# The recurrence's gate rows, made in eight pieces between the weight splits of the projection's second half

## The reference

```python
def mlstm_chunk_scan(q, k, v, li, lf, C0, n0, m0):      # per chunk of 128 tokens
        b = jnp.cumsum(fc, axis=-1)
        d_log = b[..., :, None] - b[..., None, :] + ic[..., None, :]
        inter_log = b + m[..., None]
        m_t = jnp.maximum(inter_log, jnp.max(d_log, axis=-1))
...
        m_new = m_t[..., -1]
        w = jnp.exp(b[..., -1:] - b + ic - m_new[..., None])
        decay = jnp.exp(b[..., -1] + m - m_new)
...
    li = g[:, 0]
    lf = jax.nn.log_sigmoid(g[:, 1])
```

## Time and profile before

| | |
|---|---|
| median of 3 runs | 1189.91 us (1189.72 to 1190.07) |
| profiled execution | 1190.76 us, span 1189.0 us |
| TensorE busy | 1041.1 us (88%) |
| VectorE busy | 669.0 us (56%) |
| ScalarE busy | 414.4 us (35%) |
| GpSimd busy | 202.3 us (17%) |
| mean granted TensorE clock | 0.935 of full speed |

### The profile page before, as it was taken

How to read it: one execution, slowest core, us unless ns; L and a number is a source line. 1 busy time by engine, 2 the same in 40 slices (tenths; PEclk the granted TensorE clock), 3 DMA queues, 4 the chain that set the end, 5 groups by cost and what they waited for, 6 DMA issues and landing times.

```text
span 1189.0 us, 18131 instructions
## 1 busy us (share of the span) xinstructions
PE 1041.1 (88%) x5952; PEld 795.1 (67%) x5953; DVE 669.0 (56%) x1128; ACT 414.4 (35%) x808; POOL 202.3 (17%) x244
## 2 busy tenths in 40 slices
PE   7999999999999988888878999983599999989950
PEld 3899999999999864668874555552366666556630
DVE  2544885231985158229985423357567676467644
ACT  3443222343222251546661110120344444244413
POOL 2010000000000030002363000000224443324324
PEclk9799999999999999699998999995699999989985
DMA  9634333313343132122126322217458888887839
GB/s 362 259 138 141 123 131 135 107 69 117 133 141 107 53 121 78 48 89 63 54 38 252 114 90 91 106 68 268 178 165 240 286 275 284 281 264 198 230 54 353
DMA packets 58644, 187.38 MB, mean 158 GB/s; under 512 B 7874, under 2 KB 20658, under 8 KB 52450
## 3 DMA queue, kind: packets, MB, share of 16 engines
q1 hardware_dynamic: 46820, 144.92, 34.1%
q0 software_dynamic: 7920, 28.84, 10.4%
q10 hardware_dynamic: 3856, 13.00, 2.9%
HBM read 151.53 MB, written 35.21 MB: 157 GB/s over the span
## 4 chain that ended last, share of the span: by engine, by line
PE 71%; DVE 13%; DMA 7%; issue 3%; ACT 3%; POOL 1%; ACTq 1%; SPq 0%; DVEq 0%; POOLq 0%
PE psum L1267 35%; PE psum L1209 28%; DMA RB<-in_w_exp 3%; DVE RW L1768 2%; PE psum L1486 2%; DMA RB<-in_x_sample 2%; DVE RE L1795 1%; PE psum L1132 1%; DMA acc_scratch<-RE,idxsc 1%; DMA out<-RB 1%; DVE RE L1803 1%; PE psum L1421 1%; PE psum L1224 1%; PE psum L1188 1%; DMA RW<-gm_scratch 1%
## 5 line engine op out<-in xcount | busy, mean ns | idle before, releaser
L1209 PE MATMUL psum<-input_parts,weight_parts 128*128 128x320 f32 x2208 | 342.4, 314 | 2.0 <-DVE input_parts L1591 2.0
L1209 PEld LDWEIGHTS psum<-input_parts,weight_parts 128*128 128x128 f32 x2208 | 328.4, 190 | 11.0 <-issue 6.9
L1267 PE MATMUL psum<-RB,RW 128*128 x324 | 146.5, 603 | 1.7 <-issue 1.1
L1598 DVE TENSOR_TENSOR weight_parts<-RW,weight_parts 128x1024 fp32r<-128x1024 f32 x46 | 56.3, 1224 | 155.4 <-ACT weight_parts L860 155.4
L860 ACT ACTIVATE weight_parts<-RW 128x1024 fp32r<-128x1024 f32 x46 | 48.6, 1057 | 232.8 <-PE psum L1209 232.8
L1267 PE MATMUL psum<-expert_parts 128*128 128x512 f32 x486 | 126.5, 414 | 1.9 <-DVE expert_parts L2032 1.9
L1267 PEld LDWEIGHTS psum<-expert_parts 128*128 128x128 f32 x486 | 91.3, 188 | 32.4 <-issue 14.5
L1267 PEld LDWEIGHTS psum<-RB,RW 128*128 128x128 f32 x324 | 60.7, 194 | 68.9 <-issue 68.9
L1267 PE MATMUL psum<-RS,RB 128*128 128x512 f32 (+1 forms) x200 | 79.9, 554 | 3.5 <-DMA RS<-in_wpw 2.3
L1267 PE MATMUL psum<-RC,RB 128*128 128x512 f32 x160 | 72.6, 608 | 0.0
L674 POOL TENSOR_TENSOR RE<-RE,RA 2x2304 f32<-2x2304 f32 (+1 forms) x2 | 9.5, 4762 | 361.6 <-DMA RA<-in_b_ada 361.6
(11 more groups left out here) (333 smaller groups left out, 1486.6 us busy)
## 6 DMA issues: line engine op xcount, KB each, us to landing
RB<-in_w_exp SPq DMA_DIRECT2D x48, 1024.0 KB, 7.9
RW<-in_w_in SPq DMA_DIRECT2D x46, 512.0 KB, 4.4
RW<-in_w_ada SPq DMA_DIRECT2D x34, 512.0 KB, 3.4
RA<-in_w_ada SPq DMA_DIRECT2D x10, 512.0 KB, 15.5
RW<-gm_scratch SPq DMA_DIRECT2D x20, 256.0 KB, 3.4
h_scratch<-RE SPq DMA_DIRECT2D x10, 512.0 KB, 2.6
acc_scratch<-RA SPq DMA_DIRECT2D x10, 512.0 KB, 3.6
RB<-acc_scratch ACTq DMA_DIRECT2D x10, 512.0 KB, 8.7
```

The source lines that it names most:

```text
L1209: last = nc.tensor.matmul(psum[:, 2 * r + g, 0:GW], spl[:, r, wv, k], hT[:, xv, k, g * GW:(g + 1) * GW], start=(k == 0 and wv == 0 and xv ...
L1267: return nc.tensor.matmul(out, lhsT, rhs, start=start, stop=stop, **kw_)
L1598: nc.vector.tensor_tensor(spl[:, r, 1], raw[:, r], spl[:, r, 0].bitcast(F32), ALU.subtract).then_inc(wlo_ok, 1)
```

## The change

The gate rows leave their place behind the projection. VectorE makes them in eight functions, each called between two low splits of the projection's second half; the convolution's taps start two splits later. Rows move to other memory, since their old places are in use then (`rowE`, `rowG` in the part of `RC` that later holds the second half's values, `rowF` in two slots of the projection's output, a new `rowW` in the place of the gated input). ScalarE makes the exponential and the logarithm after its second slot of the second half; it waits for all gate outputs before it evicts into `rowF`'s place, and for the stores before it writes over `rowE` and `rowG`. SP issues the stores ahead of the value chunks' weights and the load behind them. `gate_columns` stands after the second Fourier product of the sample, the second variance after the fourth. GpSimd waits for the centring as well. No step of the computation is added or left out.

```diff
@@ rows
-    rowF = RA[0:ROWG, 4 * T:5 * T]
-    rowG = RA[0:ROWG, 5 * T:6 * T]
-    rowE = RB[0:ROWG, (NSLOT + GT) * HT:(NSLOT + GT + 2) * HT]
+    rowE = RC[0:ROWG, va:va + T]
+    rowG = RC[0:ROWG, va + T:va + 2 * T]
+    rowF = RB[0:ROWG, (NSLOT + KK + 2) * HT:(NSLOT + KK + 4) * HT]
+    rowW = RB[0:ROWG, (NSLOT + GT) * HT:(NSLOT + GT + 2) * HT]
@@ sync: the six stores and the load of dec
+            if h == 1:
+                sp.wait_ge(gout, GOUT_ALL)
+                for d in range(2):
+                    sp.dma_start(gm_dram[d], rowG[32 * d:32 * d + NH, :]).then_inc(gm_out, 16)
...
             for c in range(V0, O0):
                 load_proj(None, (n0 + c) % 2, c, n0 + c - 1)
+            if h == 1:
+                sp.wait_ge(gm_out, 64)
+                sp.dma_start(dec[:, :, :, :].rearrange("p d h t -> p (d h t)"),
+                             dec_dram.rearrange("d h t -> (d h t)").partition_broadcast(P)).then_inc(dec_in, 16)
...
         sp.wait_ge(gtr_ps, 4)
+        sp.wait_ge(mrow_out, 48)
@@ gpsimd
+        gp.wait_ge(cen_ok, 4)
@@ scalar
+            if h == 1:
+                act.wait_ge(gstep, 10)
+                nc.scalar.activation(rowC, rowC, ACT.Exp, scale=-1.0).then_inc(gact, 1)
+                act.wait_ge(gact, 1)
+                nc.scalar.activation(rowC, rowC, ACT.Ln, bias=1.0).then_inc(gact, 1)
             with act.Fori(1, 3) as i:
...
+            if h == 1:
+                act.wait_ge(gout, GOUT_ALL)
+            for j in range(2):
+                slot(6, j)
...
+                if h == 1 and j == 0:
+                    act.wait_ge(gm_out, 64)
@@ tensor
-            for q, row in enumerate((LF, rowC, rowD, LI)):
+            for q, row in enumerate((LF, rowW, rowD, LI)):
...
         for i in range(TS // P):
-            if i == 6:
+            if i == 2:
                 gate_columns()
+            if i == 4:
                 variance(1)
@@ vector: the order
-        low(25, 32)
+        low(25, 26)
+        gate_logs()
+        low(26, 27)
+        gate_reversed()
+        low(27, 28)
+        gate_sums()
+        low(28, 29)
+        gate_maxima()
+        low(29, 30)
+        gate_forward()
+        low(30, 32)
         dve.wait_ge(gt_sig, 2)
         nc.vector.tensor_tensor(urest[:, :, 2 * PAD:2 * PAD + HT], PT[:, 1, CA:CA + 2], PT[:, 1, GT:GT + 2],
                                 ALU.mult).then_inc(u_ok, 1)
         dve.wait_ge(u_ok, 6)
+        gate_first()
+        low(32, 33)
+        gate_rest()
+        low(33, 34)
         first_tap(rest)
         for k in range(10):
             taps(rest, 4 * TAPS, 1 + 3 * k, 4 + 3 * k)
-            low(32 + k, 33 + k)
-        low(42, 2 * NCH)
+            low(34 + k, 35 + k)
+        low(44, 2 * NCH)
@@ vector: two of the eight pieces
+        def gate_sums():
+            link(nc.vector.memset(rowF, 1.0))
+            link(nc.vector.memset(rowF[:, 0:T:P], 0.0))
+            dve.wait_ge(gact, 2)
+            link(nc.vector.scalar_tensor_tensor(rowD, rowD, 0.0, rowC, ALU.min, ALU.subtract))
+            link(nc.vector.tensor_tensor_scan(rowC, rowF, rowD, 0.0, ALU.mult, ALU.add))
+
+        def gate_maxima():
+            dve.wait_ge(zero_out, 16)
+            link(nc.vector.tensor_tensor_scan(rowG[:, 0:TP], rowD[:, 0:TP], rowE[:, 0:TP], 0.0, ALU.add, ALU.max))
+            link(nc.vector.tensor_tensor_scan(rowG[:, TP:T], rowD[:, TP:T], rowE[:, TP:T], gvec[:, 2:3], ALU.add, ALU.max))
+            link(nc.vector.tensor_tensor(rowF, rowG, rowC, ALU.subtract))
+            link(nc.vector.tensor_tensor(rowE, rowE, rowC, ALU.subtract))
```

More of the change, by code:

```diff
@@ L417, in program @@
     GOUT_ALL = 19
+    GSTEPS = 25
     place = [2 * D, 0, 0]
@@ L524, in _ @@
         sp.dma_start(wr[:, :, :], a["w_router"]).then_inc(tab_in, 16)
-        sp.wait_ge(gout, GOUT_ALL)
-        for d in range(2):
-            sp.dma_start(gm_dram[d], rowG[32 * d:32 * d + NH, :]).then_inc(gm_out, 16)
-            sp.dma_start(dec_dram[d], small[32 * d:32 * d + NH, 3, :]).then_inc(gm_out, 16)
-            sp.dma_start(o[4][0, 0, d:d + 1, :].rearrange("a h -> h a"), small[32 * d:32 * d + NH, 2, 0:1],
-                         allow_slow_non_contiguous=True).then_inc(out_done, 16)
-        sp.wait_ge(gm_out, 64)
-        sp.dma_start(dec[:, :, :, :].rearrange("p d h t -> p (d h t)"),
-                     dec_dram.rearrange("d h t -> (d h t)").partition_broadcast(P)).then_inc(dec_in, 16)
         sp.wait_ge(gtr_ps, 4)
+        sp.wait_ge(mrow_out, 48)
         for d in range(2):
@@ L1611, in taps, with link @@
                                                    ALU.mult, ALU.add).then_inc(conv, 1)
+        steps = [0]
+        def link(ins):
+            steps[0] += 1
+            ins.then_inc(gstep, 1)
+            dve.wait_ge(gstep, steps[0])
+        SEQ = ((0, TP), (TP, T))
+        fw, bk = slice(0, NH), slice(32, 32 + NH)
+        mprev, mlast, decs, deco = (small[:, i, :] for i in range(4))
+        ch = lambda ap: ap.rearrange("p (c t) -> p c t", t=P)
+        per = lambda ap, r, c0, c1: ap[r, c0 // P:c1 // P].unsqueeze(2).broadcast_to([NH, (c1 - c0) // P, P])
@@ new lines, in gate_logs, with gate_reversed @@
+        def gate_logs():
+            dve.wait_ge(cm_ev, NCH + 1)
+            dve.wait_ge(gates_ev, 2)
+            dve.wait_ge(u_ok, 4)
+            link(nc.vector.memset(rowD, 0.0))
+            link(nc.vector.memset(rowE, 0.0))
+            link(nc.vector.tensor_copy(rowE[fw, :], LI[fw, :]))
+            link(nc.vector.tensor_scalar(rowD[fw, :], LF[fw, :], gvec[fw, 1:2], None, ALU.add))
+        def gate_reversed():
+            for c0, c1 in SEQ:
+                link(nc.vector.tensor_copy(rowE[bk, c0:c1][:, ::-1], LI[bk, c0:c1]))
+                link(nc.vector.tensor_scalar(rowD[bk, c0:c1][:, ::-1], LF[bk, c0:c1], gvec[bk, 1:2], None, ALU.add))
+            link(nc.vector.memset(rowC, 0.0))
+            link(nc.vector.scalar_tensor_tensor(rowC, rowD, -1.0, rowD, ALU.mult, ALU.max))
@@ new lines, in gate_first, with gate_rest @@
+        def gate_first():
+            link(nc.vector.memset(rowW, 0.0))
+            nc.vector.tensor_tensor(ch(rowW[fw, :]), per(mprev, fw, 0, T), ch(rowF[fw, :]), ALU.subtract).then_inc(gout, 1)
+            gate_backward(*SEQ[0])
+        def gate_rest():
+            gate_backward(*SEQ[1])
+            nc.vector.tensor_copy(deco[fw, :], decs[fw, :]).then_inc(gout, 1)
+            nc.vector.tensor_copy(deco[bk, 0:PT_TILES][:, ::-1], decs[bk, 0:PT_TILES]).then_inc(gout, 1)
+            nc.vector.tensor_copy(deco[bk, PT_TILES:][:, ::-1], decs[bk, PT_TILES:]).then_inc(gout, 1)
+            dve.wait_ge(gout, 15)
+            nc.vector.tensor_copy(decs[:, 0:1], rowG[:, TP - 1:TP]).then_inc(gout, 1)
+            dve.wait_ge(gout, 16)
+            nc.vector.tensor_scalar(rowG[fw, :], rowF[fw, :], -1.0, None, ALU.mult).then_inc(gout, 1)
+            for c0, c1 in SEQ:
+                nc.vector.tensor_scalar(rowG[bk, c0:c1][:, ::-1], rowF[bk, c0:c1], -1.0, None, ALU.mult).then_inc(gout, 1)
@@ L1713, in _ @@
-        link(nc.vector.tensor_tensor(rowF, rowG, rowC, ALU.subtract))
-        link(nc.vector.tensor_tensor(rowE, rowE, rowC, ALU.subtract))
-        mprev, mlast, decs, deco = (small[:, i, :] for i in range(4))
-        link(nc.vector.memset(mprev[:, 0:1], 0.0))
-        link(nc.vector.tensor_copy(mprev[:, 1:2], rowG[:, P - 1:P]))
-        link(nc.vector.tensor_copy(mprev[:, PT_TILES:PT_TILES + 1], gvec[:, 2:3]))
-        link(nc.vector.tensor_copy(mprev[:, PT_TILES + 1:NT], rowG[:, TP + P - 1:T - 1:P]))
@@ L1745, in _ @@
-        for c0, c1 in SEQ:
-            nc.vector.tensor_scalar(rowG[bk, c0:c1][:, ::-1], rowF[bk, c0:c1], -1.0, None, ALU.mult).then_inc(gout, 1)
         for h in range(2):
```

76 lines of the change are left out of this document (21 added, 55 removed).

## The result

The changed kernel took 1176.13 us (median of 6 runs, 1171.3 to 1181.97) where the kernel before took 1189.82 (6 runs, 1185.99 to 1190.95) beside it: a ratio of 0.9889, 95% interval 0.9866 to 0.9913. A second set gave 1180.27 (6 runs, 1177.1 to 1184.17) against 1191.65: 0.9912 (0.9885 to 0.994). The medians put the gain at 11 to 14 us; over all runs on record, 12 of the changed kernel and 64 of the one before, the means are 1178.8 and 1189.8, a gain of 11.1 us, plus or minus 2.2. Single runs of either kernel spread over more than 10 us, where the first three lay within 0.4. One run of the kernel before, in the second set, took 4848.66 us for a reason that the record does not show; no comparison uses it.

The account below looks back on a forecast made before the run. VectorE's 43 us of gate rows behind the projection were taken to hold up TensorE (88% busy) about 9 us. 9.06 + 3.85 - 1.7 + 0.8 = 12.0 us gave 1177.9 us; own range 1177.0 to 1179.2, stated range 1175.0 to 1181.6.

Parts of the forecast that it names:

- the holding clock: Rival: the clock stays up after the gate columns; gain 13.7 us, time 1176.2 us; chance 0.25.
- wait ahead of the transposes, with that for `in_wpw`: TensorE's wait before the gate columns goes, 6.24 us; the forecast counted no transfer wait.
- wait ahead of the second variance: TensorE's wait before the second variance at 483.80 goes, 2.82 us.
- transposes at full clock: The 40 gate-column transposes, 4.45 us at 1.2 GHz, take half at 2.4 GHz: 2.2 us less.
- second variance at full clock, start to start: The second variance took 4.04 us, the first 2.39 for the same eight products: 1.65 us less.
- new fall behind the transposes: The moved gate columns lower the clock once during wide Fourier products: 1.7 us lost, bounds 0 and 3.5.
- tail (1-column products, first pointwise): Half clock around the pointwise products lasts 3.3 to 6.8 us: 0.8 us gained, bounds 0 and 1.7.
- The two waits: TensorE's waits before gate columns and second variance both go: 6.24 + 2.82 = 9.06 us.
- The reason for that fall: A run of small transposes lowers the clock as 1-column products did at 497.3, though TensorE is fully busy.
- The squares: ScalarE's input to the second variance is ready near 459.7, wanted at 465.5: cover 5.8 us, no cost.
- The projection: Eight gate-row pieces fit between VectorE's low splits in the second half: cost nothing, bounds 0 and 1.0 us.
- The rival "slower": Pieces starve the projection because 4-row instructions are slow by nature: 1203 us; chance 0.03.

Follow-up runs that it names:

- Experiment 12: The kernel before, unchanged, measured and traced a second time: 1188.68 us, ratio 0.9979.
- 6: The changed kernel with its 1-column products in four groups of eight behind the fourth to seventh Fourier product: 1176.39 us, ratio 0.9893.
- 1: The changed kernel with TensorE's old order, gate columns and second variance both after the sixth Fourier product: 1178.06 us, ratio 0.9907.
- 4: The changed kernel with its first five gate-row pieces in one block ahead of low split 26: 1201.31 us, ratio 1.0127.
- experiment 3: The kernel before with GpSimd's additions made to wait for the first half's silu, their stores moved back: 1184.59 us, ratio 0.9962.
- 5: The changed kernel with ten gate-column transposes ahead of each of the second to fifth Fourier product: 1177.83 us, ratio 0.9907.
- 7: The changed kernel with transposes spread and 1-column products in groups behind the fifth to eighth Fourier product: 1175.83 us, ratio 0.989.
- 8: The changed kernel with every gate-column transpose made twice, 80 in the run for 40: 1181.23 us, ratio 0.9926.
- 10: The changed kernel with 1-column products in four groups of eight between Fourier products, a second time: 1176.02 us.
- 11: The changed kernel with transposes and 1-column products both spread, a second time: 1177.74 us.
- 2: The kernel before with TensorE's new order only, gate columns after the second Fourier product, second variance after the fourth: 1200.26 us, ratio 1.0099.

## Why the prediction was right, and where a size was off

The forecast of 1177.9 us lies between the two medians of the changed kernel, 1176.13 and 1180.27, and both are in the stated 1175.0 to 1181.6. Neither is in the 1177.0 to 1179.2 that went with the forecast itself, and the first lies on the price of a rival, the holding clock (1176.2), although the clock of that trace did not hold: a whole time can't pick the rival here. The mechanism was right. Its sum was too small: the stage gained 14.1 us, not 12.0, and that the whole time came nearer than the stage (11.1 us by the means) is in part luck. Term by term, from start to start in the two profiles:

| term | predicted | measured |
|---|---|---|
| wait ahead of the transposes, with that for `in_wpw` | 6.24 | (6.24 + 2.32) - 0.80 = 7.76 |
| wait ahead of the second variance | 2.82 | 2.82 |
| transposes at full clock | 2.2 | 4.45 - 2.61 = 1.84 |
| second variance at full clock, start to start | 1.65 | 3.88 - 2.15 = 1.73 |
| new fall behind the transposes | -1.7 | -1.8 |
| tail (1-column products, first pointwise) | 0.8 | 0.63 + 1.03 = 1.66 |
| sum | 12.0 | 14.0 |

- *The two waits.* The step "6.24 + 2.82 = 9.06" was too small by 1.5. This is the term that was mis-sized most. It read the wait of one row and left out the wait for `in_wpw` ahead of `AB` on the same engine, which lay under the same 43 us of VectorE. In the kernel before that transfer was free; now it is at the head of the chain of waits and costs 0.4 to 1.7 us. The two were to be added up and the new exposure taken off. Experiment 12 shows the sum, the chain after shows the exposure.
- *The clock.* The 40 transposes take 2.61 us at full clock, not half of 4.45: part of their time does not go with the clock. The variance was right to 0.1.
- *The fall behind the transposes.* Forecast at half probability, and it was there at the size forecast. But the rival "the clock holds" is not wrong either: in 6, 1 and 4 it held, and 4 has TensorE's order of the changed kernel to the last instruction. The prediction took for a property of the kernel what differs between executions. It also took this term and the tail for independent: where the fall stayed away (1 and 4), the low clock of the tail lasted 6.8 us again, and the loss of both together was 3.4 us all the same. The prediction had -1.7 + 0.8 for the two, the table has -0.1.
- *The reason for that fall.* The text drew it from the fall behind the 1-column products. For these the experiments bear it out: in ten traces of ten with the block, in none of four without. For the transposes it stays likely, four of seven. The Trainium skill (TensorE: Matmul & The Clock Gate, "What's actually happening") says that the clock depends on how busy TensorE has been recently. Read plainly, as the prediction read it, a TensorE without gaps keeps its clock, and that is not what these traces show: the view has it at 1.00 busy in every window of 1 us from 440 us to both falls of the changed kernel.
- *The tail.* It came at its upper bound, 1.66 for a middle of 0.8: one stretch of 3.4 us at half clock instead of 6.8. Experiments 1 and 4 have the 6.8 with the rows early as well.
- *The squares* ended at 454.4 where TensorE wanted them at 463.18: a cover of 8.8 us, 5.8 forecast. Counted from `AB`, they were ready after 26.1 us (forecast 26.8) and wanted after 34.9 (32.6), since the low clock behind the transposes and their 2.61 us for 2.2 delay the variance as well. The first pointwise product began at 482.56, not near 487.5: 3.1 us of that is the earlier start of the means, the rest the larger gain.
- *The projection.* The sums waited for ScalarE and ended at 272.64, the maxima at 279.9; the splits behind them ended 3.6 and 4.3 us ahead of the chunks at 277.46 and 285.44 (forecast 3.7 and 4.4). By the Trainium skill (SBUF — State Buffer, "Who interferes with whom") no fight with GpSimd was due there, as GpSimd does nothing then, and the 0.82 and 0.88 us agree. One small step was wrong: ScalarE's high split was to be reached 0.7 us early, and it waited for its weights instead:

```profile
266.92 1.27 ACT L917 ACTIVATE RE<-RE 36x1280 f32<-36x1280 f32 x1
269.37 1.06 ACT L865 ACTIVATE weight_parts<-RW 128x1024 fp32r<-128x1024 f32 x1 [1.18 <-DMA RW<-in_w_in]
```

  The low split behind it was kept by the sums until 272.67, so this cost nothing.
- *The rival "slower".* Its price was near: a starved projection gives 1201.3 us (experiment 4), forecast 1203. Its mechanism, instructions slow by nature, is refuted by experiment 3. What would have starved the projection is the length of a block between two splits.

Open: the whole times say 11.1 us by the means and the stage 14.1. The part from the recurrence to the end took 661.6 to 670.1 us over all traces, with no order by kernel (the changed one has 662.8 and 670.1), so a few us of either sign can come from there. The means began 2.4 to 3.1 us earlier in both traces of the changed kernel. The clock held at 235 and at 391 us there, and fell at both places, for 3.4 us each, in the traces of 1, 5 to 8, 10 and 11, whose projection is the same and whose means began at 426 to 428. So the early start belongs to these executions, not to the change; why the clock held in both of them and in none of the others is open.

## What to carry to other kernels

Work that one engine does in a block while others wait is best put into the idle slots of an earlier phase, but in pieces no longer than the room between two deadlines: five of the eight pieces in one block made TensorE wait 22.5 us, in pieces nothing. When a long block goes, look for all the waits that lay under it, not only the last: their sum is the gain, and what they hid (here a transfer) comes to light. Before moving anything, look for what makes the block long: two instructions that stood behind a neighbour engine's held 6.7 of 43 us, and making that neighbour wait gave some 40 to 55% of the stage's gain. Ask too what else raises the semaphore that an engine waits for: `AB` waits for a load that it does not read.

## What the runs showed of the hardware

- VectorE's 4-row copy and 4-row addition stood while GpSimd's additions on two partitions ran: 3.87 to 5.05 us instead of 0.81, and 4.48 to 4.50 instead of 0.87, each ending 0.67 to 0.69 us behind GpSimd's instruction in three traces (the kernel before, 2 and 12). The memset of 36 rows that began at 433.85, beside the same additions, took the 1.12 us that it takes elsewhere.
- TensorE's granted clock fell to 1.2 GHz with TensorE at 1.00 busy in the view. At or behind the 32 instructions of the one-column products in one block it fell in every trace (10 with the block), for 3.4 or 6.8 us; in four groups of eight, never (4 traces). At or behind forty 36-column transposes it fell in four of seven traces, behind eighty for 6.8 us (one trace).
- The same kernel has these falls in different places in different executions: the changed kernel with the 1-column products spread lost 0 us in one trace of the stage and 3.4 in the other.
- Forty 36-column transposes took 2.61 us at 2.4 GHz and 4.45 at 1.2 GHz, so part of their time does not follow the clock.
- Single runs of one kernel spread by 10 us and more here (64 of the kernel before: 1182.5 to 1199.0 us, mean 1189.8), so that differences under some 3 us have to be read from the stage's length in traces.
